# Three-pass products of a two-block network: moving columns and result columns addressed from last to first

## The reference

```
for each layer of the first network:
    xn = rms_norm(h);  proj = xn @ w_in            # 1024 -> some thousand columns
    mixed = recurrences on proj (gated linear attention and RWKV-7; or RG-LRU and mLSTM)
    h = h + mixed @ w_mix_out
    h = h + cross_attention(rms_norm(h), memory)   # wq, wkv, wo: 1024 x 1024 each
    h = h + (conv(silu gate) * up) @ w_down        # feed-forward, 1024 -> 2 * 2752 -> 1024
for each layer of the second network:
    x = x + even_mixer(rmsnorm(x))  or  odd_mixer(rmsnorm(x))     # spatial gating + MLA; retention
    x = x + (silu(h @ w_gate) * (h @ w_up)) @ w_down              # 1024 -> 2 * 2816 -> 1024
```

## Time and profile before

| | |
|---|---|
| median of 3 runs | 3100.71 us (3100.56 to 3102.95) |
| time of the profiled execution | 3103.16 us |
| its span, first to last instruction | 3101.4 us |
| TensorE matmul busy | 3000.0 us (97%), 17,696 records |
| VectorE / ScalarE / GpSimd busy | 1741.0 / 1272.8 / 318.6 us |
| mean granted TensorE clock | 0.99 of full speed |
| moved by DMA | 274.89 MB, mean 89 GB/s |

### The profile page before, as it was taken

The page is one execution under the profiler, slowest core; times in us unless marked ns, Lnnn a source line. Parts: engine busy times, 40 slices in busy tenths (PEclk is TensorE's granted clock), DMA queues, the critical chain, the costliest instruction groups (busy, mean ns, idle before and its releaser), DMA issues.

```text
span 3101.4 us, 41482 instructions
## 1 busy us (share of the span) xinstructions
PE 3000.0 (97%) x17696; PEld 2469.8 (80%) x17696; DVE 1741.0 (56%) x2154; ACT 1272.8 (41%) x1702; POOL 318.6 (10%) x285
## 2 busy tenths in 40 slices
PE   8988889999999999999999998999999999999999
PEld 5877678778888766778888775689998888878998
DVE  6444454547544775646544755676666453566665
ACT  5443333534322564434322545544444333344443
POOL 1010000110000100000000200124310000013240
PEclk9999999999999999999999999999999999999999
DMA  5331023223332311323332330133332222223331
GB/s 186 112 112 29 29 73 126 96 68 95 97 94 85 117 55 55 109 68 95 95 88 92 93 89 28 55 96 99 104 111 92 85 86 98 69 88 103 99 107 67
DMA packets 340104, 274.89 MB, mean 89 GB/s; under 512 B 28768, under 2 KB 308832, under 8 KB 339408
## 3 DMA queue, kind: packets, MB, share of 16 engines
q1 hardware_dynamic: 335552, 252.83, 26.5%
q0 software_dynamic: 4368, 19.41, 1.8%
HBM read 263.83 MB, written 8.39 MB: 88 GB/s over the span
## 4 chain that ended last, share of the span: by engine, by line
PE 87%; DVE 6%; ACT 5%; issue 2%; POOL 0%; DMA 0%; DVEq 0%; SPq 0%; ACTq 0%; POOLq 0%
PE ps L189 86%; ACT arena L203 2%; ACT whi L206 1%; DVE arena L220 1%; DVE arena L212 1%; DVE wlo L212 1%; PE ps L192 1%; DVE hT L212 1%; DVE xlo L220 0%; ACT L203 0%; DVE sml L229 0%; POOL arena L212 0%; ACT arena L206 0%; DVE split L212 0%; ACT split L206 0%
## 5 line engine op out<-in xcount | busy, mean ns | idle before, releaser
L189 PE MATMUL ps<-split,whi 128*128 128x512 f32 (+1 forms) x3008 | 889.6, 373 | 14.6 <-DVE hT L212 6.0
L212 DVE TENSOR_TENSOR wlo<-wraw,whi 128x2048 fp32r<-128x2048 f32 (+5 forms) x261 | 565.7, 2170 | 484.8 <-ACT whi L206 484.3
L189 PE MATMUL ps<-xhi,whi 128*128 128x512 f32 (+2 forms) x2040 | 764.7, 380 | 17.7 <-DVE xlo L212 7.2
L189 PE MATMUL ps<-xhi,wlo 128*128 128x512 f32 (+2 forms) x1984 | 741.8, 374 | 0.0
L189 PE MATMUL ps<-xlo,whi 128*128 128x512 f32 (+2 forms) x1944 | 729.9, 376 | 0.0
L189 PEld LDWEIGHTS ps<-split,whi 128*128 128x128 f32 x3008 | 549.4, 189 | 131.4 <-issue 25.0
L206 ACT ACTIVATE whi<-wraw 128x2048 fp32r<-128x2048 f32 (+5 forms) x261 | 456.9, 1754 | 337.3 <-PE ps L189 237.0
L189 PE MATMUL ps<-split,wlo 128*128 128x512 f32 (+1 forms) x1504 | 554.6, 369 | 0.0
L189 PEld LDWEIGHTS ps<-xhi,whi 128*128 128x128 f32 (+1 forms) x2040 | 381.7, 189 | 101.6 <-issue 14.6
L189 PEld LDWEIGHTS ps<-xhi,wlo 128*128 128x128 f32 (+1 forms) x1984 | 374.2, 189 | 69.0 <-issue 5.1
L189 PEld LDWEIGHTS ps<-xlo,whi 128*128 128x128 f32 (+1 forms) x1944 | 365.7, 188 | 67.9
(11 more groups left out here) (132 smaller groups left out, 2432.7 us busy)
## 6 DMA issues: line engine op xcount, KB each, us to landing
wraw<-in_ffn_w_up SPq DMA_DIRECT2D x128, 512.0 KB, 4.8
wraw<-in_odd_w_in SPq DMA_DIRECT2D x24, 1024.0 KB, 5.0
wraw<-in_ffn_w_gate SPq DMA_DIRECT2D x44, 512.0 KB, 3.7
wraw<-in_ffn_w_down SPq DMA_DIRECT2D x20, 1024.0 KB, 5.0
wraw<-in_ffn_w_down SPq DMA_DIRECT2D x24, 768.0 KB, 4.4
wraw<-in_xattn_wkv SPq DMA_DIRECT2D x16, 1024.0 KB, 5.5
wraw<-in_xattn_wq SPq DMA_DIRECT2D x8, 1024.0 KB, 5.0
wraw<-in_xattn_wo SPq DMA_DIRECT2D x8, 1024.0 KB, 5.0
```

The costliest lines, as they stand in the source:

```text
L189: return self.e.matmul(out, lhsT, rhs, start=start, stop=stop, skip_group_check=True)
L212: return self.e.tensor_tensor(out, a, b, op)
```

## The change

`mm3` makes reversed views of its moving operand and of its result and passes these to the three matmuls. The access pattern of both had 512 elements with a step of +1 and starts at column 0; it now has 512 elements with a step of -1 and starts at column 511. The stationary operand is untouched. Since both are reversed, column t of the result is still computed from column t of the activations, and it lies where it lay.

```
-            pe.mm(out, hi, src.hi[0:rows, :], start, False)
-            pe.mm(out, lo, src.hi[0:rows, :], False, False)
-            return pe.mm(out, hi, src.lo[0:rows, :], False, stop)
+            x_hi, x_lo, y = src.hi[0:rows, ::-1], src.lo[0:rows, ::-1], out[:, ::-1]
+            pe.mm(y, hi, x_hi, start, False)
+            pe.mm(y, lo, x_hi, False, False)
+            return pe.mm(y, hi, x_lo, False, stop)
```

## The result

The changed kernel takes 3142.93 us (median of 4 runs, 3139.61 to 3146.76) against 3100.64 us (4 runs, 3099.13 to 3102.95): a ratio of 1.0135, 95% interval 1.0123 to 1.0147, so 42 us slower. The prediction's likeliest case, no change (3,094 to 3,108 us), did not come; the small price per matmul (rival C, 3,110 to 3,187) did.

What follows compares the result with a forecast made beforehand. TensorE's dense matmul stream was taken as the bound; all four parts priced 0 left the profiled 3,103 us, 3,101 as a median (no change, 0.53). Own range 3,094 to 3,108, stated range 3,090 to 4,870 (0.92).

Steps and rivals of the forecast that it cites:

- rival C: Reversed matmuls: a start price of 1 to 10 ns for patterns ending below their start; 3,110 to 3,187 us; chance 0.05.
- rival A: Every `mm3`: write or read side takes descending columns singly, half pace, +0.200 us a matmul; 4,811 us; chance 0.24.
- What bounds the kernel: TensorE's dense `mm3` stream, 0.2270 us a matmul; 8,568 rewritten matmuls, 63% of the span, almost wholly on the path.
- Part (1): Instructions, queues, waits: none added, removed or moved, no DMA touched, readers and accumulation keep their timing; price 0.
- Part (2): Moving operand read from column 511 down; gapped reads at 0.233 us taken as nearest evidence; price 0.
- break-even: Smallest change the measurement can tell: about 0.2%, 6.2 us, which is 0.7 ns a matmul over 8,568.
- Part (3): Result written from column 511 down and added there; no row bears on it, the less certain half; price 0.
- Part (4): The 384 matmuls of 256 columns, 0.12 us apart: price 0, or +0.093 us each at one column every other cycle.
- Rival B: Descending matmuls must finish before the next starts: 0.39 us in place of 0.227; about 4,480 us; chance 0.10.
- D: Fast float32r mode lost, reversed matmuls run as plain float32: +0.678 us each, about 8,900 us; chance 0.03.
- E: Faster: the 13.7 ns a matmul over one column a cycle vanish, 117 us less, 2,984 us; chance 0.05.

Runs made afterwards that it cites:

- e2: Against the kernel before, the three passes write the result from column 511 down, reads still upwards: 3102.62 us against 3102.85, ratio 1.0002.
- m4: Streams alone, 512 columns, no kernel: moving operand shifted by 8 columns 233.4 ns a matmul, weights shifted by 8 233.2, both together 226.9.
- m5: Streams alone, moving operand fixed, weights shifted by 0 to 60 columns: upwards 226.7 ns at 0, 233.2 at 8; downwards 233.3 to 236.6.
- e7: Kernel before, nothing reversed, weights' buffers 32 bytes further on, activations and working area in place: 3143.51 us against 3101.29, ratio 1.0133.

## Why the prediction was right or wrong

The measured 3,142.93 us lies inside the stated range of 3,090 to 4,870, but by luck and not by the mechanism: the upper end was put there for rival A, which did not come, and the forecast's own range of 3,094 to 3,108 misses the time by 35 us.

- **What bounds the kernel.** Right. The dense stream's 0.227 us decides, and the price of one matmul arrived in the time, three quarters of it.
- **Part (1), no order, wait or queue changes.** Right. The chain gained in TensorE's share, 85.7 to 87.9%, and no new wait appears.
- **Part (2), the reads.** This step failed: "I take 0". It measured +6.6 ns in a dense stream (6.1 as the mean of all close starts). I rested it on gapped reads the earlier trace rows, 0.233 us each, and put the 6 ns over 0.227 down to rounding or to the jumps. Either way they were read from three matmuls, and a price of just this size was within their scatter; the same rows were named as the nearest and then taken as evidence for nothing. The trace holds 24 such reads, and the 17 that follow each other closely have a mean of 230.8 ns (224 to 236), 3.5 over unbroken ones, so they did not stand for a price of 0 (whether the 3.5 come from the jumps or from the place of the weights is open). What the step left out is that the pace hangs on where the moving read stands against the weights within 256 bytes and on the order inside such a stretch. The break-even that the prediction itself gave, 0.7 ns, was about a tenth of what the three printed rows could resolve.
- **Part (3), the writes.** Price 0, right (e2). I had called it the less certain half; the certain half was the wrong one.
- **Part (4), 256 columns.** Price 0 was nearly right: alone in a stream it is -1.5 ns, at 384 matmuls 0.6 us, too small to be seen in the time.
- **Rival A, half pace.** Refuted by both one-sided kernels. It had 0.24.
- **Rival B, overlap lost.** Refuted: durations of 0.40 us at distances of 0.23.
- **Rival C, a price of 1 to 10 ns.** It is what came, with a chance of 0.05 much too small. Its size was right, its mechanism not: the price isn't that of a pattern which ends below its start, since two halves and blocks of 64 do that too and cost nothing in the full kernel, and since at 256 columns there is none.
- **Rivals D and E.** Out. D's price was also read too high: the 1.81 us of the earlier trace rows run to the start of the next operation, while the four records start 0.43 us apart, 0.86 us a matmul, so +0.633 and not +0.678. E put the 13.7 ns over one column a cycle down to a conflict that another first column avoids; at 512 columns no place and no direction that was tried came below 226.7 ns.

## What to carry to other kernels

In a float32r stream of 512 columns with 128x128 weights a matmul costs 226.7 ns at best and mostly 233.3 otherwise. The direction of the moving read and the distance of the two operands in SBUF, taken within 256 bytes, decide: read upwards, or at least in blocks of 64 columns or more, and let the two operands start a multiple of 256 bytes apart. Where the pair stands as a whole did not matter (moved together by 32 bytes, it cost nothing). At 256 columns the same rule does not hold, so measure other lengths anew.

Between a negligible and a huge price lies the small one per instruction; where an edit touches thousands of instructions of a saturated engine, a few ns each need a chance of their own. A bench of streams must hold the distance of its operands fixed, or it measures its own allocation.

## What the runs showed of the hardware

- The write pattern of a matmul may run from last to first, or in blocks of 2 or 4 columns from last to first, at no price (226.7 to 226.9 ns).
- Moving reads of every second float32r column halve the pace (453 ns, measured with the operands 128 bytes out of step, which elsewhere cost under 7 ns). The Trainium skill (SBUF — State Buffer, Specifications (TRN2)) holds that two hits on a 16-byte line keep full bandwidth; every second float32 column has two hits, and the measurement says otherwise for this operand. By the same rule the prediction had descending reads, with four hits on a line, at no price; they cost 6.6 ns.
- The Trainium skill (SBUF — State Buffer, Who interferes with whom) gives TensorE two independent read ports, one for the moving operand and one for weights, and lets it wait on nobody. Here the distance of the two operands costs 6.5 ns a matmul, in streams (m4, m5) and in the kernel (e7). That is hard to square with two wholly independent reads; the meeting itself is inferred, and no trace shows it.
- The reversal costs nothing at half the clock: close starts are 426.0 ns apart before (granted clock 0.50) and 425.3 after.
- What stays open: what meets in the memory, why the downward read finds no free distance at 512 columns, why fewer weight columns make upward reads dearer, and what else counts at other lengths (448 columns upwards: 206.5 and 202.7 ns at the same distance within 256 bytes). At 256 columns only the distances 0, 8 and 32 were tried, and for other data types none but 0.
